# Memory's keys and values inside the sample recurrence, attention's heads interleaved with the samples', turned tiles in preparation

## The reference, cut to what matters

```
m = rmsnorm(mem_prompt, g);  mem_k = m @ w_k;  mem_v = m @ w_v      # 256 x 1024 -> 4 heads x 128
# RWKV: k, v, r, decay, a, b from token-shifted projections; S is 64 x 64 for each of 8 heads
S = S * w + (S a) b + v k ;  y = S r                                # prompt: chunks of 64; samples: 4 tokens
y = (head_layernorm(y) * ln_w + ln_b + bonus) * g
# attention, 4 heads of 128: prompt on mem_k, mem_v; each sample on its own cached keys and values
s = q . k * 128 ** -0.5;  p = softmax(s);  y_xa = p @ v
```

## Time and profile before

| | us |
|---|---|
| median of 3 runs | 2667.21 (2660.73 to 2667.88) |
| profiled execution | 2662.08 |
| its span | 2660.3 |
| mean granted clock of TensorE | 0.939 |

### The profile page before, as it was taken

The page is one execution under the profiler, slowest core; times in us unless marked ns, Lnnn a source line. Parts: engine busy times, 40 slices in busy tenths (PEclk is TensorE's granted clock), DMA queues, the critical chain, the costliest instruction groups (busy, mean ns, idle before and its releaser), DMA issues.

```text
span 2660.3 us, 41336 instructions
## 1 busy us (share of the span) xinstructions
PE 2383.6 (90%) x16321; PEld 2195.8 (83%) x16321; DVE 1722.8 (65%) x3186; ACT 914.0 (34%) x1569; POOL 693.2 (26%) x1003
## 2 busy tenths in 40 slices
PE   7976796887668989989899987999999999999997
PEld 5954675875546978888799987999999999999996
DVE  3545376434642444448979987887786478878876
ACT  2222243210111111112234355777784333333332
POOL 3300000011430555425521200333333032332330
PEclk9987898996886999999999989999999999999999
DMA  4520320013752899757775746999999799999993
GB/s 145 185 57 11 113 56 17 20 43 104 242 182 99 281 289 302 242 171 252 231 239 192 240 154 187 319 336 317 323 323 360 266 326 348 343 348 343 350 346 116
DMA packets 323185, 586.48 MB, mean 220 GB/s; under 512 B 26704, under 2 KB 217184, under 8 KB 321456
## 3 DMA queue, kind: packets, MB, share of 16 engines
q1 hardware_dynamic: 222960, 274.07, 31.5%
q0 software_dynamic: 81600, 282.49, 30.9%
q10 hardware_dynamic: 18432, 27.27, 2.8%
HBM read 455.09 MB, written 128.64 MB: 219 GB/s over the span
## 4 chain that ended last, share of the span: by engine, by line
PE 44%; DVE 13%; DMA 10%; ACT 3%; POOL 2%; issue 2%; ACTq 0%; DVEq 0%; POOLq 0%
PE PS L1075 43%; DMA u_rows<-arena 3%; DVE LO L2146 2%; DMA RAW<-in_uT 2%; DMA u_rows<-CBLK 2%; DMA GU<-u_rows,EIDX 2%; DVE OH L2279 2%; POOL u_rows L537 2%; DVE GU L2288 2%; ACT OH L1017 1%; ACT HI L979 1%; DVE arena L2243 1%; DVE arena L1677 1%; DVE arena L2234 1%; DVE arena L1638 1%
## 5 line engine op out<-in xcount | busy, mean ns | idle before, releaser
L2146 DVE TENSOR_TENSOR LO<-RAW,HI 128x1024 fp32r<-128x1024 f32 x256 | 313.1, 1225 | 234.5 <-ACT HI L979 233.8
L979 ACT ACTIVATE HI<-RAW 128x1024 fp32r<-128x1024 f32 x256 | 270.3, 1056 | 551.5 <-PE PS L1075 503.7
L1075 PE MATMUL PS<-HT,W 128*128 128x272 f32 (+1 forms) x1536 | 374.9, 405 | 18.5 <-DVE HT L1689 12.5
L1075 PE MATMUL PS<-XH,HI 128*128 128x416 f32 x1024 | 369.8, 361 | 10.1 <-issue 8.4
L1075 PEld LDWEIGHTS PS<-HT,W 128*128 128x128 f32 (+1 forms) x1536 | 292.2, 192 | 94.8 <-issue 18.4
L1075 PE MATMUL PS<-XH,LO 128*128 128x416 f32 x1024 | 364.1, 356 | 0.0
L1075 PE MATMUL PS<-WH,HI 128*128 128x416 f32 x1024 | 360.4, 352 | 1.4 <-DVE WL L2161 1.4
L1075 PE MATMUL PS<-XL,HI 128*128 128x416 f32 x1024 | 361.6, 353 | 0.0
L1075 PE MATMUL PS<-WL,HI 128*128 128x416 f32 x1024 | 359.6, 351 | 0.0
L1075 PE MATMUL PS<-WH,LO 128*128 128x416 f32 x1024 | 357.4, 349 | 0.0
L1075 PE MATMUL PS<-arena 64*64 64x64 f32 (+10 forms) x3864 | 275.0, 261 | 49.8 <-DVE arena L1638 23.6
(11 more groups left out here) (262 smaller groups left out, 3639.8 us busy)
## 6 DMA issues: line engine op xcount, KB each, us to landing
RAW<-in_uT SPq DMA_DIRECT2D x128, 512.0 KB, 5.3
RAW<-in_vT SPq DMA_DIRECT2D x128, 512.0 KB, 5.7
arena<-in_uT POOLq DMA_DIRECT2D x90, 512.0 KB, 5.3
W<-in_w_in SPq DMA_DIRECT2D x58, 512.0 KB, 5.4
u_rows<-arena POOLq DMA_DIRECT2D x216, 128.0 KB, 4.0
table_a<-AX ACTq DMA_DIRECT2D x128, 208.0 KB, 4.6
gate_table<-GST SPq DMA_DIRECT2D x13, 2048.0 KB, 13.7
AIN<-table_a SPq DMA_DIRECT2D x128, 208.0 KB, 6.7
```

Source lines behind the costliest of these rows:

```text
L979: nc.scalar.activation(HI[:, s % NRING], RAW[:, s % NRING], ACT.Copy).then_inc(S("hi"), 1)
L1075: return nc.tensor.matmul(out, lhsT, rhs, start=first, stop=last)
L2146: dve.tensor_tensor(LO_[:, s % NRING], RAW[:, s % NRING], HI[:, s % NRING].bitcast(F32), ALU.subtract).then_inc(S("lo"), 1)
```

## The change

Memory's norm, keys and values move from behind barrier 2 into the sample recurrence: `ms1` before the state products, `mk0` to `mk3` each ahead of a state update, `mv0` and `mv1` behind the last. The memory and its norm lie in the branch buffer `BR`, free at that point; keys and values get a place of their own at the arena's end. The load is issued on GpSimd's queue once the last prompt output is made. In the weight stream the keys' and values' columns go ahead of the queries'.

In attention all four heads have their own `PA`, key cache and value cache, each cache loaded by two transfers of 2 MB; the samples' scores are placed between the heads' products. VectorE's and ScalarE's programs follow that order. The samples' probabilities have a buffer `PD`, and the masks of a head release that head's value products.

The tiles: phases S and A go; P is new (11 tiles in preparation, two buffers), R has 7, N stays at 8, with buffers of its own. In phases with two buffers the stores of a tile now go ahead of the next load.

```diff
-TILES = {"M": (0, 10, 1), "R": (10, 4, 1), "S": (14, 2, 2), "N": (16, 8, 2), "A": (24, 12, 2), "G": (36, 58, 2),
+TILES = {"M": (0, 10, 1), "P": (10, 11, 2), "R": (21, 7, 1), "N": (28, 8, 2), "G": (36, 58, 2), "Q": (94, 26, 2),
...
-    o += ["abs", "nts", "is1", "is2", "vts", "bts", "us", "uus", "ys"] + [f"ss{p}" for p in range(RP)]
+    o += ["abs", "nts", "is1", "is2", "vts", "bts", "ms1", "us", "uus", "ys"]
+    for p in range(RP):
+        o += [f"mk{p}", f"ss{p}"]
+    o += ["mv0", "mv1"]
...
-    o += ["ms1"] + [f"mk{h}" for h in range(MH)] + ["mv0", "mv1", "as0"]
-    for h in range(MH):
-        o += ([f"as{h + 1}"] if h + 1 < MH else []) + [f"at{h}", f"ao{h}"]
-    o += [f"ds{h}" for h in range(MH)] + ["dt"] + [f"do{h}" for h in range(MH)]
+    o += ["as0", "as1", "as2", "at0", "ds0", "ao0", "as3", "at1", "ds1", "ao1", "ds2", "at2", "ds3", "ao2", "at3", "ao3",
+          "dt"] + [f"do{h}" for h in range(MH)]
...
-    s += [(f"xq{h}", "w_in", 0, DT, OFF_XQ + h * P, P, f"xq{h}") for h in range(MH)]
     s += [(f"mk{h}", "w_mk", 0, DT, h * P, P, f"mk{h}") for h in range(MH)]
     s += [(f"mv{c}", "w_mv", 0, DT, c * P, P, "mv1") for c in range(4)]
+    s += [(f"xq{h}", "w_in", 0, DT, OFF_XQ + h * P, P, f"xq{h}") for h in range(MH)]
...
# GpSimd
+                    if depth == 1:
+                        load_tile(phase, i)
                     if k >= first:
...
+                    if depth == 2:
+                        load_tile(phase, i)
...
+            turn_tiles("P")
             turn_tiles("R")
+            pool.wait_ge(mm, NO[f"y{NC - 1}"] + 1)
+            pool.dma_start(MEM, a["memT"].rearrange("(k p) t -> p k t", p=P)).then_inc(S("in0"), 16)
...
-            turn_tiles("S")
             pool.wait_ge(mm, NO[f"ss{RP - 1}"] + 1)
-            pool.dma_start(MEM, a["memT"].rearrange("(k p) t -> p k t", p=P)).then_inc(S("in0"), 16)
             turn_tiles("N")
...
             for r in range(2):
-                if r:
-                    turn_tiles("A")
...
+                pool.dma_start(KB[:, 2 * r:2 * r + 2], a["memkT"][:, 2 * r:2 * r + 2]).then_inc(S(f"ldk{r}"), 16)
+            for r in range(2):
+                pool.dma_start(VBM[:, 2 * r:2 * r + 2], a["memv"][:, 2 * r:2 * r + 2]).then_inc(S(f"ldvv{r}"), 16)
...
# VectorE, preparation
             for i in range(5):
                 shift(i)
+                turn_tile("P")
...
                     shift(6 + 3 * p)
+                    turn_tile("P")
...
                     shift(7 + 3 * p)
+                    turn_tile("P")
...
# VectorE, prompt's recurrence
                 chunk_state(c)
+                turn_tile("R")
...
-                turn_tile("R")
+                if more:
+                    turn_tile("R")
...
# VectorE, sample recurrence
             dve.sem_inc(S("svbk"), 1)
-            turn_tile("S")
+            dve.wait_ge(S("in0"), 48)
+            norm(1, MEM, MN, "mem_norm", NMEM)
             ps = take(dve, "us")
...
# VectorE, attention (new order)
+            below_max(0)
+            below_max(1)
+            normalise(0)
+            below_max(2)
+            sample_scored(0)
+            normalise(1)
+            below_max(3)
+            sample_scored(1)
+            normalise(2)
+            sample_scored(2)
+            sample_scored(3)
+            below_max(MH)
+            normalise(3)
+            normalise(MH)
...
# ScalarE, sample recurrence
             act.wait_ge(S("in0"), 48)
             f(MN, MEM, ACT.Square, S("sq"))
             root(1, NMEM)
+            sample_outputs()
```

More of the change, by code:

```diff
@@ L77 @@
 NCBLK = 2088
+AFTER_YQ = 20800
+MEMKV = 25088
 AREN = 28400
@@ L180, in tile_chunk, with tile_stores @@
     return i if i < E_FROM else i + n
+def tile_stores(phase, i):
+    first, n, _ = TILES[phase]
+    return 64 * ((first + n + 1 - i) // 2)
 def part_slot(t, part):
@@ L348, in hybrid_layer @@
         chunk_rest = BR[:, 4:12].rearrange("p a b -> p (a b)")[:, 3 * D:4 * D]
[L349 to L354, removed]
+        before_chunks = [BR[:, 4:12].rearrange("p a b -> p (a b)")[:, i * D:(i + 1) * D] for i in range(4)]
+        beside_norm = [arena[:, AFTER_YQ + i * D:AFTER_YQ + (i + 1) * D] for i in range(4)]
+        tile_in = {"M": [arena[:, low:low + D]], "P": before_chunks[0:2], "R": [chunk_rest], "N": beside_norm[0:2],
+                   "G": [arena[:, low - D:low], arena[:, low:low + D]], "Q": [TQ[:, 0], TQ[:, 1]]}
+        tile_out = {"M": [top], "P": before_chunks[2:4], "R": [arena[:, AREN - D:AREN]], "N": beside_norm[2:4],
+                    "G": [top, CBLK[:, NCBLK - D:NCBLK]], "Q": [TQ[:, 2], TQ[:, 3]]}
         tile_out["E"] = tile_out["Q"]
@@ L522, in fill, with load_tile @@
                 step(pool.memset(tile, value))
+            def load_tile(phase, i):
+                first, n, depth = TILES[phase]
+                if i < first + n and phase != "E":
+                    pool.dma_start(tile_in[phase][(i - first) % depth],
+                                   a["uT"][:, tile_chunk(i)].rearrange("p k n -> p (k n)")).then_inc(S(f"tin{i % 2}"), 16)
             def turn_tiles(phase):
@@ L859, in _ @@
                     inverse_copy(c, i)
+            for i in range(2):
+                act.wait_ge(S(f"tout{i}"), tile_stores("P", i))
             for i in range(NC // 2):
@@ L871, in _ @@
                 nxt(8)
-            sample_outputs()
-            for p in range(RP):
-                both(f"xq{p}", XQ[:, p, :], ACT.Copy, S("xq"))
-                act.wait_ge(S("yv"), p + 1)
-                f(rstd[:], rstd[:], ACT.Sqrt, S("ysq"))
-            barrier(act, 2)
             act.wait_ge(S("in0"), 48)
@@ L890, in _, with probs_turned @@
                 act.sem_inc(S("mkv"), 1)
+            for p in range(RP):
+                both(f"xq{p}", XQ[:, p, :], ACT.Copy, S("xq"))
+                act.wait_ge(S("yv"), p + 1)
+                f(rstd[:], rstd[:], ACT.Sqrt, S("ysq"))
+            barrier(act, 2)
             def exponentials(h):
                 act.wait_ge(S("sx"), h + 1)
-                f(PA[:, h % 2], PA[:, h % 2], ACT.Exp, S("sxe"), scale=SCALE)
-            exponentials(0)
-            for h in range(MH):
-                if h + 1 < MH:
-                    exponentials(h + 1)
+                x = PA[:, h] if h < MH else PD
+                f(x, x, ACT.Exp, S("sxe"), scale=SCALE)
+            def probs_turned(h):
                 ps = take(act, f"at{h}")
@@ L1395, in _ @@
             ins.then_inc(mm, 1)
+            pe.wait_ge(S("sq"), 3)
+            ps = room("ms1")
+            for k in range(DT):
+                ins = mul(ps[:, 0, 0:NMEM], ones[:], MN[:, k, :], k == 0, k == DT - 1)
+            ins.then_inc(mm, 1)
             pe.wait_ge(S("svbk"), 1)
@@ L1421, in _ @@
             ins.then_inc(mm, 1)
+            pe.wait_ge(S("hn"), 2 * DT)
             for p in range(RP):
+                w = weights(f"mk{p}")
+                ps = room(f"mk{p}")
+                for k in range(DT):
+                    ins = mul(ps[:, 0, 0:NMEM], w[:, k, :], MN[:, k, :], k == 0, k == DT - 1)
+                ins.then_inc(mm, 1)
                 pe.wait_ge(S("uve"), p + 1)
@@ L1427, in _ @@
                               UVE[0:2 * TS, x].rearrange("p a b -> p (a b)"))
+                ins.then_inc(mm, 1)
+            for s in range(2):
+                ps = room(f"mv{s}")
+                for c in range(4):
+                    w = weights(f"mv{c}")
+                    for k in range(DT):
+                        ins = mul(ps[:, 0, c * P:(c + 1) * P], MN[:, k, s * P:(s + 1) * P], w[:, k, :],
+                                  k == 0, k == DT - 1)
                 ins.then_inc(mm, 1)
@@ L1471, in memory_scores, with probs_turned @@
                 ins.then_inc(mm, 1)
-            memory_scores(0)
-            for h in range(MH):
-                if h + 1 < MH:
-                    memory_scores(h + 1)
+            def probs_turned(h):
                 pe.wait_ge(S("soft"), h + 1)
@@ L1931, in chunk_state @@
                 tt(new, new, bc(WE[:, :, c], 2, RD), sem=S("stnew"))
+            for i in range(2):
+                dve.wait_ge(S(f"tout{i}"), tile_stores("P", i))
             for c in range(2):
```

154 lines of the change are left out of this document (73 added, 81 removed).

## The result

The kernel before took 2664.12 us (2660.73 to 2667.88, 4 runs), the changed one **2622.87 us** (2621.56 to 2624.73, 4 runs): a ratio of 0.985 [0.983, 0.9869]. The forecast was 2611 in a range of 2595 to 2631, and it was made on a median of 2667.2. As a difference it said -56.3 us; measured are -41.3 us in the medians and -38.7 us in the spans of the profiled executions (2660.3 to 2621.6). The 15 us between are what has to be explained. The measured median lies inside the stated range, but outside the 2605 to 2618 that the prediction gave to its own forecast.

What follows compares the result with a forecast made beforehand. It summed stretches, not any engine's share; in attention TensorE and VectorE each wait for the other. Terms 4.0 + 0 + 13.9 - 0.5 - 73.7 = -56.3 us from 2667.2 gave 2610.9, say 2611, range 2595 to 2631.

Steps and rivals of the forecast that it cites:

- Attention: Barrier 2 to the next stage: work moved out and heads overlapping samples' scores give 74.9 us, a gain of 73.7.
- one of the two signs by which the prediction would call itself wrong: Wrong if the state products wait for the memory's load, or if attention's value products change pace from 27.7 us.
- Rival B: Attention's heads stay a chain of 14.0 us each, 17 us worse: 2628 us, chance 0.23.
- Keys and values in the sample recurrence: Memory's sum, keys and values on TensorE before normalisation, which begins at 657.4 instead of 643.5: +13.9 us.
- no delay to the state products: Sample recurrence: memory's sum product fits TensorE's idle time in 3.45 us, ending at 604.0 to 604.5, without delaying state products.
- rival A: TensorE's clock rises through the sample recurrence behind dense products: -7.4 us, 2603 us, chance 0.18.
- Normalisation: First round starts at the upper clock, its projection 7.5 instead of 8.41 us: -0.5 us; other rounds stay.
- Preparation: Eleven added tiles on VectorE, mostly hidden; those in the loop cost 3 x 1.27 + 0.15 = +4.0 us.
- everything later is untouched: The change lies between barrier 1 and 852 us; no term was given for the stages after that.
- no wait: Normalisation, two buffers: store first delays the load 2.2 us, landing after about 8.4, needed after 11.1, so no wait.
- Rival C: Tiles starve in preparation, holding in-order VectorE 13.1 us each, 79 us: 2690 us, chance 0.02.
- Rival D: No change: the moved work costs 56 us on TensorE, only if attention kept its length: 2667 us, chance 0.02.

Runs made afterwards that it cites:

- e6: Changed kernel with memory's norm, keys and values back behind barrier 2, heads and samples still interleaved: 2652.61 us, ratio 0.9958 of the kernel before.
- e7: Changed kernel with attention's heads one after another and the samples' scores behind the last head: 2646.46 us, ratio 0.9929 of the kernel before.
- e1: The changed kernel run again without an edit, as the foot for other runs: 2621.92 us, ratio 0.9854 of the kernel before.
- e5: Changed kernel with loads issued ahead of stores in the gate stage's phase alone: 2611.99 us, ratio 0.9804 of the kernel before.
- e8: Changed kernel with loads ahead of stores, preparation's tile ahead of VectorE's wait, sample state's store ahead of normalisation's tiles: 2602.51 us, ratio 0.9754.
- e4: Changed kernel with preparation's tile behind shift 6+3p moved ahead of the wait for ScalarE's root: 2617.94 us, ratio 0.9835 of the kernel before.
- e2: Changed kernel with the load again ahead of the four stores in all two-buffer phases: 2608.17 us, ratio 0.9799 of the kernel before.

## Why the prediction came out as it did

**Attention, right (-73.8 measured, -73.7 said), for the reason given, to the tenth by luck.** Its schedule held step by step. From the barrier the first head's transposes ended at 13.8 us (13.6 said), the second's at 23.5 (23.7), the third's at 33.6 (31.9), the fourth's at 42.6 (40.6), and the value products began at 48.9 (46.8). They took 25.5 instead of 27.7, which happened to pay for the 2 us. That change of pace was one of the two signs by which the prediction would call itself wrong, and it came: the first 6.6 us of them ran at a mean granted clock of 0.67, the rest at 0.50. e6 and e7 show the two causes separately: back behind the barrier, keys and values cost 44 us of attention, and in turn the heads cost 21.6. The 8 us that are left of the 73.8 (the twelve tiles that went, and the order of the caches' loads) no run has taken apart. Rival B, that the heads stay a chain, is what e7 builds; in the changed kernel it does not happen, since TensorE has other heads' and samples' scores to do.

**Keys and values in the sample recurrence, near in the sum (+13.9 said, +14.5 with the 0.3 ahead of it), by luck.** That the sum product causes "no delay to the state products" was wrong. The sum product took 5.41 us, as at 705.35 and at a mean granted clock of 0.68, not 3.45, and e6 against e1 prices it at 3.9 us of TensorE's path (163.9 to 167.8). Only 0.3 us of it can be seen against the kernel before, because the profile of that kernel had ten slow microseconds at the end of the prompt's recurrence, which the changed kernel's profile did not have (before, then changed):

```profile
586.85:596.85 10.00, 7.48 (x150) 6.96 (x146) 4.44 (x8) 0.38 (x1) 2.17 (x4) 0.67 0.23 56
```

```profile
585.52:595.52 10.00, 6.98 (x218) 6.52 (x214) 3.37 (x6) 1.36 (x3) 4.15 (x8) 1.00 0.53 154
```

TensorE's last transposes ahead of the sum product ended 162.9 us after the chunks began in the one and 159.1 in the other. Where both came together, the slow stretch and the sum product (e5, e7, e8), the stage took 171.1 to 171.6 us.

Behind the sum product the 144 state products ran in 5.48 us at a granted clock of 1.00, where the earlier trace rows had them at 65 ns each. That is rival A's mechanism at one place: they now stand right behind dense work. e6 shows it from the other side, 9.45 us behind 4.75 us of idleness. But only 1.5 of these 3.9 us reached the outputs: the state products ended at 618.8 and VectorE took them at 620.8, when memory's norm was off its hands; the prediction had the two meet. Rival A had more in it, too, which did not come: the outputs still took 7.89 us at 0.50, and the value products of attention ran at a mean granted clock of 0.54 (0.50 before) with TensorE busy for 25.5 of 25.9 us. The Trainium skill's rule that sustained activity of the array releases the clock (TensorE: Matmul & The Clock Gate, Part 1) agrees with the state products and not with the outputs and the value products; the trace decides, and it says both.

**Normalisation, right in mechanism, small in size (-0.5 said, -2.05 measured).** The first round starts at the upper clock: 1.08 and 7.50 us for its first two groups. e6, which starts it from the lower clock, has 2.18 and 8.44. The forecast counted only the second group, the projection; with the first it is 1.10 + 0.94 = 2.04.

**Preparation, a mis-sized term (+4.0 said, +7.0 measured).** The term was "3 x 1.27 + 0.15 = +4.0 us", and it is right for VectorE: the tile does stand in its chain. What it left out is TensorE's next projection, which ran 1.7 us slower in two rounds, at a mean granted clock of 0.82, behind a gap that had grown by 1.1 us; a round took 30.8 us, not 29.2. The prediction named the projection that waits and did not ask what clock it would find. e4 takes away both parts at once, and in its profile preparation is 152.7 us again.

**Behind barrier 3, the step that failed.** The prediction said "everything later is untouched", and of the phases of depth 2 that "a store now goes ahead of the next load, which delays the load by 2.2 us; it then lands about 8.4 us behind the tile that freed its buffer, which is needed again after 11.1: no wait". The arithmetic is right for normalisation, the one phase it was applied to. The same two lines of the helper serve the 58 tiles that begin with the gate stage and the top-k stage's 26. In the gate stage VectorE waits already, before the change at 45 of the 50 tiles that it turns there, and so has nothing under which 2.2 us could go. There the order cost 8.5 to 11.4 us (254.3 in e2 and e5 against 262.8 and 265.7 with the stores first), and in all 13.75 us by e2; how much of the rest belongs to the top-k stage is open. With the 13.7 us of the two stages the sum of the prediction comes to 42.6 us under the time before; 41.3 were measured. That this is so close is again partly luck: preparation cost 3.0 us more than said, and normalisation 1.6 less.

Rival C, tiles that starve in preparation, did not come. Rival D is excluded by the interval.

## What to carry to other kernels

A helper that several stages call is changed in all of them: before calling a stage untouched, look for the edited lines in every caller, and there for the wait that they feed. In a queue shared by loads and stores, the order that suits a stage is read from what its consumer waits for: where it waits for neither, the order is free; where it waits at each tile, the order decides whether it waits for the load or for the stores, and here the load first was the cheaper one. An instruction that is to fill idle time belongs ahead of the wait, not behind it; behind it, it is part of the chain however short, and on TensorE's side the delay can cost more than its own length. What a piece costs is best read against the same kernel without that piece, as e6 does for the sum product: against the one profile of the kernel before, a slow stretch elsewhere hid all but 0.3 of its 3.9 us.

## What the hardware showed unexpectedly

- Behind a gap of 2.90 us 32 products of 128x272 took 9.26 us (granted clock 0.82), behind one of 1.73 to 1.77 us 7.57 (1.00). 1.1 us of delay cost 2.8.
- 144 products on a 64x32 part of the array took 5.48 us straight behind 16 products of 128x256 (granted clock 1.00), and 9.45 behind 4.75 us of idleness (0.52).
- The value products, 128 of 128x128 by 128x32, took 25.5 to 27.8 us (25.52 in the changed kernel, 27.51 in e7, 27.71 before) without a gap in them, at a mean clock of 0.50 before and 0.54 in the changed kernel: a busy engine does not by itself show the upper clock.
- The prompt's recurrence, up to the end of the samples' transposes, whose code is the same in all kernels but for the tiles, took 159.1 to 164.0 us. In the kernel before, e5, e7 and e8 (162.7 to 164.0) ten microseconds near its end ran at a granted clock of 0.66 or 0.67, in the changed kernel and e6 (159.1 and 159.2) at 1.00. No run here tells what decides it.
